# HGRN score passes behind whole projection units: a reordering of TensorE's queue in a two-layer hybrid mixer kernel

## The reference

```python
h = rms_norm(x, mix_norm[layer])
c_rwkv, c_dil, c_mla, c_hgrn = split_cols(h @ w_in[layer], MIXER_COLS)
y_a = rwkv7_time_mix(c_rwkv, ...)
y_b = dilated_attention(...)
y_c = mla_attention(c_mla, ...)
y_d = hgrn2_mixer(c_hgrn, lower_bounds[layer], hgrn_g_norm[layer])
x = x + jnp.concatenate([y_a, y_b, y_c, y_d], axis=-1) @ w_out[layer]
```

```python
forget = lb + (1.0 - lb) * jax.nn.sigmoid(z)
log_f = jnp.log(forget)
k = 1.0 - forget
o = gated_linear_recurrence_chunked(heads(jax.nn.silu(q)), k, heads(i), log_f)
```

## Time and profile before

| what | value |
|---|---|
| median of three runs | 1797.98 us (1790.87 to 1803.89) |
| the profiled execution, device time | 1798.41 us |
| its span, first to last instruction | 1796.5 us |
| mean granted TensorE clock | 0.957 |
| PE busy | 1674.1 us, 93% |
| DVE busy | 1349.1 us, 75% |
| ACT busy | 1061.2 us, 59% |
| POOL busy | 131.3 us, 7% |

### The profile page before, as it was taken

How to read it: one execution, slowest core, us unless ns; L and a number is a source line. 1 busy time by engine, 2 the same in 40 slices (tenths; PEclk the granted TensorE clock), 3 DMA queues, 4 the chain that set the end, 5 groups by cost and what they waited for, 6 DMA issues and landing times.

```text
span 1796.5 us, 27016 instructions
## 1 busy us (share of the span) xinstructions
PE 1674.1 (93%) x9570; PEld 1426.0 (79%) x9570; DVE 1349.1 (75%) x1286; ACT 1061.2 (59%) x1039; POOL 131.3 (7%) x151
## 2 busy tenths in 40 slices
PE   5979888999798898799999999999999999999997
PEld 4867677999797776778788788888888788888886
DVE  3887655454458765688888788888888888888885
ACT  3532444344344334477677677677677677777775
POOL 1052100000004310000000100000000100000000
PEclk8989988999898996799999999999999999999999
DMA  6520034653352101489999999999999999999993
GB/s 204 165 83 24 16 100 161 208 171 133 94 164 79 55 1 32 156 289 366 339 331 367 339 327 368 310 366 359 316 367 351 316 366 341 327 369 352 328 368 121
DMA packets 326320, 427.99 MB, mean 238 GB/s; under 512 B 6800, under 2 KB 293680, under 8 KB 326144
## 3 DMA queue, kind: packets, MB, share of 16 engines
q1 hardware_dynamic: 325488, 425.28, 70.4%
q0 software_dynamic: 640, 2.00, 0.4%
q10 hardware_dynamic: 144, 0.05, 0.0%
HBM read 426.25 MB, written 1.05 MB: 238 GB/s over the span
## 4 chain that ended last, share of the span: by engine, by line
PE 77%; DVE 10%; ACT 4%; DMA 4%; issue 4%; SPq 0%; DVEq 0%; ACTq 0%; POOL 0%; POOLq 0%
PE bank L368 31%; PE bank L393 14%; PE bank L1077 11%; PE bank L621 7%; PE bank L371 7%; PE bank L396 4%; DMA ring<-in_moe_w 3%; ACT wh L428 1%; PE bank L381 1%; DVE wl L432 1%; DMA ring<-in_w_in 1%; PE bank L1082 1%; ACT mh L602 1%; DVE ml L608 1%; DVE proj L1667 1%
## 5 line engine op out<-in xcount | busy, mean ns | idle before, releaser
L432 DVE TENSOR_TENSOR wl<-ring,wh 128x2048 fp32r<-128x2048 f32 x369 | 845.8, 2294 | 213.8 <-ACT wh L428 200.6
L428 ACT ACTIVATE wh<-ring 128x2048 fp32r<-128x2048 f32 x369 | 706.7, 1915 | 132.6 <-PE bank L393 45.5
L368 PE MATMUL bank<-wh,xh 128*128 128x512 f32 x896 | 361.8, 404 | 4.7 <-DVE xl L828 4.7
L368 PE MATMUL bank<-wh,xl 128*128 128x512 f32 x896 | 350.9, 392 | 0.0
L368 PE MATMUL bank<-wl,xh 128*128 128x512 f32 x896 | 349.2, 390 | 0.0
L368 PEld LDWEIGHTS bank<-wh,xh 128*128 128x128 f32 x896 | 168.2, 188 | 43.5 <-issue 10.8
L368 PEld LDWEIGHTS bank<-wh,xl 128*128 128x128 f32 x896 | 168.1, 188 | 37.6
L368 PEld LDWEIGHTS bank<-wl,xh 128*128 128x128 f32 x896 | 168.7, 188 | 32.1
L393 PE MATMUL bank<-wh,gh 128*128 128x512 f32 x448 | 175.3, 391 | 4.3 <-DVE gl L518 4.3
L393 PE MATMUL bank<-wl,gh 128*128 128x512 f32 x448 | 174.4, 389 | 0.0
L393 PE MATMUL bank<-wh,gl 128*128 128x512 f32 x448 | 174.4, 389 | 0.0
(11 more groups left out here) (281 smaller groups left out, 2480.2 us busy)
## 6 DMA issues: line engine op xcount, KB each, us to landing
ring<-in_moe_w SPq DMA_DIRECT2D x336, 1024.0 KB, 8.2
ring<-in_ffn_w SPq DMA_DIRECT2D x33, 1024.0 KB, 5.9
ring<-in_w_in SPq DMA_DIRECT2D x24, 1024.0 KB, 5.4
ring<-in_w_out SPq DMA_DIRECT2D x8, 1024.0 KB, 5.2
ring<-in_w_in SPq DMA_DIRECT2D x2, 640.0 KB, 4.1
const<-in_const SPq DMA_DIRECT2D x1, 1266.5 KB, 12.2
proj<-in_x SPq DMA_DIRECT2D x1, 1024.0 KB, 5.1
out<-wide SPq DMA_DIRECT2D x1, 1024.0 KB, 4.0
```

The costliest lines, as they stand in the source:

```text
L368: ins = nc.tensor.matmul(up_bank(run, par, 0)[:], x[:, 0:C], w[b][:, k], **kw)
L428: nc.scalar.activation(o, src[0], ACT.Copy).then_inc(sem("w_high"), 1)
L432: nc.vector.tensor_tensor(split(wl[:, buf]), src[0], split(wh[:, buf]).bitcast(F32), ALU.subtract).then_inc(sem("w_split"), 1)
```

## The change

Each half-and-half interleaving is replaced by a whole unit with its passes behind it. The order on PE becomes 9a, 9b, S1, S2, rotary partners, 10a, 10b, S3, S4, 11a, 11b, S5, S6, 12a, 12b with L1124, S7, crossed. Nothing is added or removed on any engine; the queues of DVE, ACT, POOL and SP stay as they are. The argument `parts` of `unit` goes.

```diff
-            def unit(layer, u, parts=(0, 1)):
+            def unit(layer, u):
                 slot, b = u % RING_M, u % 2
                 _, cols, token_major = UNITS[u]
-                if u >= 2 and 0 in parts:
+                if u >= 2:
                     pe.wait_ge(sem("unit_copied"), layer * NU + u - 1)
-                for part in parts:
+                for part in range(2):
                     if u == 0:
                         pe.wait_ge(sem("x_split"), x_before(layer, 0) + part + 1)
                     ins = pe_unit_half(pe, layer, u, part, bank[b], not token_major)
                     if part == 0:
                         ins.then_inc(sem("half_used"), 1)
-                if 1 not in parts:
-                    return
                 if u == NU - 1:
...
                 hgrn_scores(0)
-                for u, (early, late) in ((9, (1, 2)), (10, (3, 4)), (11, (5, 6)), (12, (7, None))):
-                    unit(layer, u, (0,))
-                    hgrn_scores(early)
-                    unit(layer, u, (1,))
-                    if late:
-                        hgrn_scores(late)
+                for u, levels in ((9, (1, 2)), (10, (3, 4)), (11, (5, 6)), (12, (7,))):
+                    unit(layer, u)
+                    for e in levels:
+                        hgrn_scores(e)
                     if u == 9:
```

## The result

The changed kernel took 1806.17 us (median of 15 runs, 1799.81 to 1818.0) against 1797.98 us (15 runs, 1790.87 to 1803.89): ratio 1.0054, 95% interval 1.0037 to 1.0072, so 6.7 to 12.9 us slower. Its profiled execution took 1811.3 us, 12.9 more than the profiled one of before, with a span of 1809.4 us and a mean granted clock of 0.949 (before 0.957).

The account below looks back on a forecast made before the run. In the edited stretch the bound was the chain alternating between PE and DVE, through crossed. Delays of 3.5 us in layer 1 and 2.2 in layer 0, together 5.7 on 1798.41, gave 1804; range 1795 to 1812.

Parts of the forecast that it names:

- Each mask that loses its cover costs 1.84 us of PE standing still: Between neighbouring passes on PE: 2.93 us from pass to pass, of which the pass is 1.09, leaving 1.84 us idle.
- Part 1: S1 moves behind half 9b: DVE's own queue covers the later scores, S2 starts as before, cost nothing.
- Parts 2 and 3: S3 behind half 10b, S5 behind 11b: S4 1.84 us later, DVE's queue late, S6 1.7 us later.
- Part 4: S7 moves behind unit 12 and L1124: mask 7 is in the open before crossed, 1.84 us more.
- Layer 1: 3.5 us, layer 0: 2.2: Delay up to crossed per layer; layer 0 has 2.2 if S6 restarts at full clock, 3.5 if slowly again.
- Behind crossed all is as before, only later: Stretches after crossed: they keep their lengths and only move later with crossed; no further cost.
- more slow restarts: Rival: new waits before S4, S6 and crossed each restart PE slowly, 8.1 us on top of 5.7: 1812; chance 0.2.
- A wait of 1.87 us at 154.32, was followed by a full-speed group: PE's row nearest to the expected 1.9 us wait before S6: the group behind it took 1.16 us.
- I take the full clock: S6 in layer 0 was assumed to restart at full clock, without the 1.35 us price of a slow restart.
- A rule weighed: Skill rule that frequent PE micro-idles make the clock fall; weighed for three breaks per layer, adding nothing by the 1.87 us row.
- The delay is absorbed: Rival: a transfer or DVE queue behind crossed is later anyway, so the time stays at 1798; chance 0.1.
- faster: Rival: earlier `unit_used` of unit 10 starts the chain 1.09 us sooner per layer, S6 at full speed: 1795; chance 0.04.

Follow-up runs that it names:

- E5: Kernel before, order untouched, with eight extra 128x128 matmuls that nobody reads in front of crossed in both layers: 1814.02 us, ratio 1.0082.
- E9: Kernel before with the extra matmuls of E5 and filler matmuls in front of PE's waits from `vtok` on: 1787.65 us, ratio 0.9933.
- E1: Kernel before with only unit 9 kept whole, so that only S1 moves behind half 9b: 1805.91 us, ratio 1.0042.

## Why the prediction came out as it did

The time lay in the range and the direction was right. The mechanism was right only in part, and that the number came out near is luck: in the profiled pair the forecast 5.7 us up to crossed were -0.3, and 14.7 us were lost where none was forecast.

**"Each mask that loses its cover costs 1.84 us of PE standing still":** right as a wait. Passes are 2.90 us apart against 2.93 forecast, before S4, S6 and crossed alike.

**Part 1, "cost nothing":** mis-sized, a gain of 0.8 us a layer up to S2. "S2 starts as before" took DVE's queue as fixed; its products shortened when POOL's level 2 moved out from beside them. The wait before S2 shrank from 2.28 to 1.74 in layer 1, where 2.3 to 2.6 were forecast.

**Parts 2 and 3, S6 1.7 us later:** from S4 to S6 it is 10.25 us against 10.52 before, where the forecast had 10.4; the arithmetic of DVE's late queue held.

**Part 4, 1.84 us before crossed:** S6 to crossed took 10.61 us where 10.95 was forecast and 9.11 was before.

**"Layer 1: 3.5 us, layer 0: 2.2":** measured +0.5 and -0.8 from S0 to crossed. Layer 1 shows why: S2 and what follows restarted at the lower clock before and at full clock after, so S2 to S3 took 8.76 us where 7.49 + 3.07 was to be expected, 1.8 less, and S2 came 0.8 earlier. In layer 0 S2 to S3 took 10.40 us, 1.6 less than 8.89 + 3.07, and S6 restarted at full clock, as forecast. The slow restart before S6 was priced; that the one before S2 could go was not.

**"Behind crossed all is as before, only later":** this is the step that failed. In the profiled pair 14.7 us were lost between `vtok` and `w_out`, more than the 12.9 of the whole, without a new wait there. The rival "more slow restarts" had the right cause but the wrong place: it looked only at PE's new waits, and none of the passes behind them was slow in the profiled execution. The largest loss came in a stretch that the change doesn't touch and that it only shifts. E5 shows that a shift suffices, E5 with E9 that most of what it costs goes when PE is kept at work there. Why a shift of a few microseconds decides whether the clock falls at the start of the solve or only near its end or behind it is open; nothing here ties it to one wait. E1, whose solve in layer 1 came at about the same time as before, shows that the length of the shift alone doesn't foretell it.

**"A wait of 1.87 us at 154.32, was followed by a full-speed group":** true of that group alone. The next two ran at 1.58 and 1.91 us, where layer 1 has 1.12 and 1.04, so the clock fell right behind the row that was taken for a full-speed restart. That wait goes both ways, as the one of 2.25 us does, and the row was no ground for "I take the full clock". That S6 then ran at full clock is luck as far as these rows go.

**A rule weighed.** The "psum-queue depth-cycling" rule of the Trainium skill (page "TensorE: Matmul & The Clock Gate", section "A second HAM failure mode: psum-queue depth-cycling") was set aside on the strength of that one row. (The rival that it points to is the first of the list, not the third.) In the solve the clock fell with no wait of PE longer than 0.85 us just ahead, which is what the rule describes: many small breaks between short groups. The trace agrees with it there, at 5.4 to 6.0 us a layer, and not at the breaks for which it was weighed. The same breaks stood in the solve before, where the clock stayed at 1.00 and 0.95, so the rule doesn't tell which of the two will happen.

**"The delay is absorbed" and "faster":** neither. The expert stretch kept its length (1056.8 us from the router to the end, 1056.3 after).

## What to carry to other kernels

A reordering is priced in two places: in its own stretch, and wherever a chain of small matmuls waits on other engines and its granted clock is at one level in one layer or run and at the other in the next, for a shift there can cost more than the edit. Find such stretches first, by windows with the granted clock beside the length, and hold PE at work in them with matmuls in front of its waits; that gained 0.9% here, made the runs tighter (1780.9 to 1783.25 us, where before spread over 14 us), and only then did the parts come near the whole. When parts don't add up to the whole, look for a state that they all touch. And when a row is read for the clock, read the two groups behind it as well.

## What the hardware showed beyond that

- The filler is more than free where PE waits: 51 more matmuls a layer (3, 2, 6 and 40), and `vtok` to `w_out` is 2.3 and 7.3 us shorter than before.
- A DVE product of two 128x512 tiles took 0.69 us alone and 1.20 with POOL at work on `hk` and `hend`. It isn't so each time: at 591.35 us of the changed kernel such a product took 0.69 us beside POOL, and it was POOL's multiplication of only 128x16 on `hend` that took 0.74, where one of 128x128 had taken 0.40 at 575.52.
- In twelve profiled solves without filler the length was 12.9 us six times and 17.6 to 19.0 the other six (and 18.5, 18.6 in E5); with filler it was 12.9 in all fourteen.
- After one and the same wait of PE (1.86 or 1.87 us, before the pass on `rha,kha`) the two groups behind that pass took 1.12 and 1.04 us in one layer and 1.58 and 1.91 in the other, in one execution of the kernel before.
